# A two-block model on one core: the stick-breaking heads dealt among the portions of dense work, and the masked copy of the scores joined with its maximum

## What is computed

```python
def _stick_breaking_mixer(h, w_in, w_out):       # h: 256 x 1024, w_in: 1024 x 3072, w_out: 1024 x 1024
    q, k, v = [a.reshape(B, S, H, DH) for a in jnp.split(h @ w_in, 3, axis=-1)]     # 8 heads of 128
    z = jnp.einsum('bqhd,bshd->bhqs', qc, k) * scale
    mask = s_idx[None, :] < t[:, None]
    log_beta = jax.nn.log_sigmoid(z)
    log_one_minus = jnp.where(mask, jax.nn.log_sigmoid(-z), 0.0)
    between = lax.cumsum(log_one_minus, axis=3, reverse=True) - log_one_minus
    a = jnp.where(mask, jnp.exp(log_beta + between), 0.0)
    return (a @ v) @ w_out
```

## Time and profile before

| | us |
|---|---|
| median of 3 runs | 3481.79 (3479.11 to 3485.41) |
| profiled execution: its own time | 3479.61 |
| its span (first to last instruction) | 3477.9 |
| PE busy in it | 3281.5 (94%) |
| DVE, ACT, POOL busy | 1991.3, 1636.0, 205.3 |

### The profile page before, as it was taken

One profiled execution on the slowest core, in us unless ns is written; L12 is line 12 of the kernel. 1 busy time (PEld: TensorE's weight loads), 2 busy tenths in 40 slices (PEclk: granted clock), 3 DMA queues, 4 the chain that ended last, 5 costly groups with the idle time before them and its releaser, 6 DMA issues.

```text
span 3477.9 us, 51810 instructions
## 1 busy us (share of the span) xinstructions
PE 3281.5 (94%) x19397; PEld 2849.5 (82%) x19397; DVE 1991.3 (57%) x2821; ACT 1636.0 (47%) x2448; POOL 205.3 (6%) x247
## 2 busy tenths in 40 slices
PE   6998999998999999999998999899969998999899
PEld 5976988976988978898976987688758877887797
DVE  5555556565556656556655556755545555555663
ACT  4444444444444445444444445544444446445553
POOL 1010001000001000101011001000001000101100
PEclk9998999999999999999998999899989999999999
DMA  6653556542555643555653655145505550555364
GB/s 205 193 184 98 182 187 188 186 156 86 170 184 181 193 157 105 162 192 179 193 185 97 199 182 183 49 162 189 179 33 167 190 170 1 170 182 168 111 200 152
DMA packets 405035, 551.98 MB, mean 159 GB/s; under 512 B 33936, under 2 KB 247008, under 8 KB 404864
## 3 DMA queue, kind: packets, MB, share of 16 engines
q1 hardware_dynamic: 401056, 536.10, 47.9%
q0 software_dynamic: 2976, 10.81, 0.9%
q10 hardware_dynamic: 832, 2.74, 0.2%
HBM read 548.47 MB, written 1.05 MB: 158 GB/s over the span
## 4 chain that ended last, share of the span: by engine, by line
PE 84%; DVE 10%; ACT 3%; issue 1%; DMA 1%; POOL 0%; SPq 0%; DVEq 0%; ACTq 0%
PE G L768 15%; PE G L772 15%; PE G L769 15%; PE G L869 10%; PE G L871 10%; PE G L870 10%; DVE ring_lo_sb L1814 4%; PE T L744 2%; PE G L1250 1%; PE O L993 1%; PE S L965 1%; DVE act_hi_sb L1828 1%; DVE act_lo_sb L1838 1%; ACT ring_hi_sb L1317 1%; DVE x_sb L1996 0%
## 5 line engine op out<-in xcount | busy, mean ns | idle before, releaser
L1814 DVE TENSOR_TENSOR ring_lo_sb<-ring_sb,ring_hi_sb 128x1024 fp32r<-128x1024 f32 (+1 forms) x996 | 1207.9, 1228 | 661.0 <-ACT ring_hi_sb L1317 641.7
L1317 ACT ACTIVATE ring_hi_sb<-ring_sb 128x1024 fp32r<-128x1024 f32 (+1 forms) x1028 | 1060.6, 1045 | 792.3 <-DMA ring_sb<-ffn_w_down 223.9
L869 PE MATMUL G<-act_hi_sb,ring_hi_sb 128*128 128x256 f32 x3072 | 855.1, 278 | 0.0
L871 PE MATMUL G<-act_hi_sb,ring_lo_sb 128*128 128x256 f32 x3072 | 853.0, 278 | 0.0
L870 PE MATMUL G<-act_lo_sb,ring_hi_sb 128*128 128x256 f32 x3072 | 852.9, 278 | 0.0
L768 PE MATMUL G<-ring_hi_sb,hid_hi_sb 128*128 128x512 f32 x1456 | 586.1, 403 | 17.5 <-DVE hid_hi_sb L1847 5.1
L769 PE MATMUL G<-ring_lo_sb,hid_hi_sb 128*128 128x512 f32 x1456 | 582.1, 400 | 0.0
L871 PEld LDWEIGHTS G<-act_hi_sb,ring_lo_sb 128*128 128x128 f32 x3072 | 576.5, 188 | 0.0
L869 PEld LDWEIGHTS G<-act_hi_sb,ring_hi_sb 128*128 128x128 f32 x3072 | 576.5, 188 | 0.0
L870 PEld LDWEIGHTS G<-act_lo_sb,ring_hi_sb 128*128 128x128 f32 x3072 | 576.5, 188 | 0.0
L772 PE MATMUL G<-ring_hi_sb,hid_lo_sb 128*128 128x512 f32 x1344 | 534.6, 398 | 0.0
(11 more groups left out here) (243 smaller groups left out, 2533.8 us busy)
## 6 DMA issues: line engine op xcount, KB each, us to landing
ring_sb<-ffn_w_gate_up SPq DMA_DIRECT2D x704, 256.0 KB, 3.9
ring_sb<-ffn_w_down SPq DMA_DIRECT2D x352, 256.0 KB, 3.7
ring_sb<-mlp_w_up SPq DMA_DIRECT2D x256, 256.0 KB, 3.7
ring_sb<-mlp_w_down SPq DMA_DIRECT2D x256, 256.0 KB, 3.7
ring_sb<-a_w_in SPq DMA_DIRECT2D x48, 256.0 KB, 4.0
ring_sb<-sb_w_in SPq DMA_DIRECT2D x48, 256.0 KB, 4.1
ring_sb<-moba_w_in SPq DMA_DIRECT2D x48, 256.0 KB, 4.0
ring_sb<-w_mem_kv SPq DMA_DIRECT2D x32, 256.0 KB, 4.1
```

Of the source, the lines that this page charges most:

```text
L869: mm(dst, hi, act_hi[:, kt, :], start=(kt == 0 and f == 0), stop=False, skip_group_check=True)
L871: last = mm(dst, lo, act_hi[:, kt, :], start=False, stop=(kt == KT - 1), skip_group_check=True)
L1317: fn(ring_hi[:, s_, :, 0:w], ring[:, s_, :, 0:w], ACT.Copy).then_inc(hi_ready, 1)
L1814: v.tensor_tensor(ring_lo[:, s_, :, 0:w], ring[:, s_, :, 0:w], ring_hi[:, s_, :, 0:w], ALU.subtract).then_inc(lo_ready, 1)
```

## The change

1. **The stick stage becomes a `fused` one.** `FUSED_CHUNKS["stick"]` has the two chunks of values first (row-major, as before) and then four chunks that hold queries and keys of two heads each. These four are computed with the weights stationary (`turned_cell`), so queries and keys stand channel-major in `proj` and are used from there: the transposes and ACT's copies of them fall away. Chunk 2 comes ahead of the heads, chunks 3, 4, 5 in steps 0 to 5, the output projection from step 6 on (`DEAL["stick"]`), four cells per step. Heads still go in pairs. In an even step PE does the sums (`remaining`) of the last two heads, then the scores of the next; in an odd step its scores and then both outputs of the last pair.
2. **Its tiles shrink to 128 x 384** (`TRI`), without the part that is masked away; the sums go to the PSUM banks of the transposes (`T`); the multiplication L2429 goes.
3. **`score` is joined**: one `tensor_tensor_reduce` per half of the rows, out = (scores + mask) * (-scale), with the minimum as second output; two per head in place of four (masked) or two (unmasked). ACT takes exp with scale -1. POOL negates the scale for normed heads with one more instruction (`rsqrt(..., negative=True)`).
4. **`split_limits`**: in the last three steps of every fused stage the limit is max(touched[last], the last limit) + 1 and no longer the last limit + 3. This gives 27, 28, 29 where 29, 32, 32 stood for mix_b; 31, 32, 33 for 31, 34, 36 in mix_c and moba; 39, 40, 41 for 41, 44, 44 in nsa.
5. nsa: the multiplication with `cmp_any` moves out of each head's `place` (L2045, 8 times) to one place ahead of the heads (2 instructions).

```diff
+            "stick": [[(2 * D, HALF)], [(2 * D + HALF, HALF)]] + [[(p * GRP, GRP), (D + p * GRP, GRP)] for p in range(4)],
...
+        DEAL["stick"] = [("in", 2, BOTH, -1, -1), ("in", 3, BOTH, 0, 1), ("in", 4, BOTH, 2, 3), ("in", 5, BOTH, 4, 5),
+                         ("out", 0, BOTH, 6, 6), ("out", 1, BOTH, 6, 6), ("out", 2, BOTH, 7, 7), ("out", 3, BOTH, 7, 7),
+                         ("out", 4, BOTH, 8, 8), ("out", 5, LOWER, 8, 8), ("out", 5, UPPER, 9, 9)]
+        TRI = SEQ + P
...
-                limits.append(min(touched[min(s + 2, last)], full) if s < last - 2 else min(full, limits[-1] + 3))
+                limits.append(min(touched[min(s + 2, last)], full) if s < last - 2
+                              else min(full, max(touched[last], limits[-1]) + 1))
...
+                def turned_cell(j, par, slot, u):
+                    for k in range(UNIT_K):
+                        kt = UNIT_K * u + k
+                        for f in range(2):
+                            wide = slice((2 * j + f) * P, (2 * j + f + 1) * P)
+                            to, hi, lo = G[:, j, par, f * SEQ:(f + 1) * SEQ], ring_hi[:, slot, k, wide], ring_lo[:, slot, k, wide]
+                            mm(to, hi, act_hi[:, kt, :], start=(kt == 0 and f == 0), stop=False, skip_group_check=True)
+                            mm(to, hi, act_lo[:, kt, :], start=False, stop=False, skip_group_check=True)
+                            last = mm(to, lo, act_hi[:, kt, :], start=False, stop=(kt == KT - 1), skip_group_check=True)
+                    return last
+                def remaining(h):
+                    prepared()
+                    bank, j = t_open(c["T"]), h % 2
+                    mm(bank[:, 0:SEQ], from_on, pt[:, j, 0:SEQ], start=True, stop=False, skip_group_check=True)
+                    mm(bank[:, P:SEQ], ones, pt[:, j, SEQ:TRI], start=False, stop=True, skip_group_check=True)
+                    mm(bank[:, SEQ:TRI], from_on, pt[:, j, SEQ:TRI], start=False, stop=True, skip_group_check=True)\
+                        .then_inc(t_full, 1)
...
+                def stick_step(step):
+                    past = [step // 2 * 2 - 2, step // 2 * 2 - 1] if step >= 2 else []
+                    if step % 2 == 0:
+                        for h in past:
+                            remaining(h)
+                    if step < n_heads:
+                        if "taken" in heads[step]:
+                            for t in range(TT):
+                                pe.wait_ge(g_taken[t], g + heads[step]["taken"])
+                        stick_score(step)
+                    if step % 2:
+                        for h in past:
+                            stick_weigh(h)
...
+                for t in range(TT):
+                    w = N_CMP if h["k"][0] == "cmp" else P if h["mask"] and t == 0 else SEQ
+                    dst, src, top = sc[:, b, t, 0:w], S[:, t, 0:w], mx[:, col + t:col + t + 1]
...
+                    ins = v.tensor_tensor_reduce(dst, src, add, scales[t], BIG, ALU.add, ALU.min, top)
                 ins.then_inc(s_taken, 1)
                 dve.wait_ge(s_taken, base + j + 1)
-                v.tensor_reduce(mx[:, col:col + TT], dst, AX_X, ALU.max, negate=True)\
-                 .then_inc(mx_ready, 1)
+                dve.sem_inc(mx_ready, 1)
...
                     if step < n_steps:
                         ahead(n + limits[step])
                         finished(cut[step])
+                    if kind == "stick":
+                        stick_last(step)
```

More of the change, by code:

```diff
@@ L41 @@
 NEG = -1e30
+BIG = 3e38
 SCALE1 = DH1 ** -0.5
@@ L692, in plan @@
                 return mem + hs
+            if kind == "stick":
+                return [dict(taken=3 + h // 2) if h % 2 == 0 else {} for h in range(H2)]
             if kind == "moba":
@@ L1116, in fused @@
                     dense(lead)
-                for step in range(n_heads + 4):
+                for step in range(steps_of(kind, n_heads)):
+                    if kind == "stick":
+                        stick_step(step)
+                        dense(cut[step])
+                        turn_y(step)
+                        continue
                     if step < n_heads:
@@ L1500, in fused @@
                         hooks[step, "sums"]()
-                    if 0 <= step - 1 < n_heads:
+                    if 0 <= step - 1 < n_heads and kind != "stick":
                         exps(heads[step - 1], step - 1, base)
@@ L1760, in _ @@
                     per = -(-CONV_W // DIAGS)
-                    c["mixf"] = H2 * sum(k == "stick" for k, *_ in stages[:s]) + sum(k == "mix_a" for k, *_ in stages[:s])
+                    c["mixf"] = sum(k == "mix_a" for k, *_ in stages[:s])
                     for g in range(2, len(diag_groups) + per):
@@ new lines, in stick_last @@
+                def stick_last(step):
+                    if step % 2 and step < n_heads:
+                        for h in (step - 1, step):
+                            sc_ = sc[:, h % 2, :, :].rearrange("p t n -> p (t n)")[:, 0:TRI]
+                            dve.wait_ge(fn_out, c.up("fn_out"))
+                            v.scalar_tensor_tensor(pt[:, h % 2, 0:TRI], sc_, 0.0, pt[:, h % 2, 0:TRI], ALU.max,
+                                                   ALU.add).then_inc(prep_ready, 1)
@@ new lines, in fused @@
+                n_steps = steps_of(kind, n_heads)
+                for step in range(n_steps + 1):
+                    if kind == "stick":
+                        stick_first(step) if step < n_steps else None
+                    else:
+                        if 0 <= step - 1 < n_heads:
+                            score(heads[step - 1], step - 1, base)
+                        if step < n_heads and turns(heads[step]):
+                            c.up("T")
+                        if 0 <= step - 3 < n_heads:
+                            c.up("T")
+                        if kind == "mix_c" and step == 2:
+                            c.up("T")
+                        if 0 <= step - 4 < n_heads:
+                            place(heads[step - 4], step - 4, base)
+                    if step < n_steps:
@@ L2401, in lead @@
                     dve.wait_ge(fn_out, c.up("fn_out"))
+                    for t in range(TT):
+                        ins = v.tensor_scalar(gates[:, t, 0:H2], gates[:, t, 0:H2], cmp_any[:, t:t + 1], None, ALU.mult)
+                    link(ins)
                     done()
```

275 lines of the change are left out of this document (117 added, 158 removed).

## The result

The changed kernel's median is 3433.95 us (4 runs, 3424.85 to 3437.46) against 3483.6 for the kernel before (4 runs, 3479.11 to 3488.7): a ratio of 0.9847, 95% interval 0.9823 to 0.987. Timed again on another chip it gave 0.9859 (0.9835 to 0.9882). The profiled execution took 3433.15 us, with a span of 3431.3. That is 1.5% faster, 50 us, where 61 were forecast.

What follows compares the result with a forecast made beforehand. PE, busy 94% of the span, bounds the kernel, leaving its waits and lower-clock stretches; gains 40.6 + 11.7 + 4 + 6 - 1 = 61.3 us off 3479.6 give 3418.3, median 3420 us, range 3402 to 3444 (own range 3405 to 3434).

Steps and rivals of the forecast that it cites:

- Stick: Stick stage: falls from 166.1 to 125.5 us, a gain of 40.6 us (36 to 47).
- logs and banks: Stick steps 2, 4, 6: PE waits for `stick_last` and a bank, 5.0 us together; step 8 for the bank, 0.7.
- output copies: Stick steps 3, 5, 7: the second output waits 1.1 us each for DVE; step 9 waits 0.6.
- step 0's copy: Stick step 0: PE waits 1.0 us for the copy of chunk 2.
- last turn: Stick's last turn of the result: PE waits 1.6 us for ACT and DVE.
- opening and splits: Stick's opening and the splits of chunk 2: 2.5 us of waiting.
- second rival: Stick: splits in DVE's queue hold PE up, three times 5 us plus clock; stage 147, total about 3442; chance 0.18.
- long chain through ACT: Stick, between scores and sums: about 4.9 us through DVE and ACT, hidden under 7.5 us of PE work.
- Limits: Ends of nsa, mix_b, moba, mix_c: fewer splits ahead save 4.6, 4.6, 1.5, 1.0 us; gain 11.7 (0 to 14).
- Clock: Nsa and mix_b: with waiting gone, part of the time at 1.2 GHz goes too; gain 4 us (0 to 8).
- Joined scores: 72 heads outside stick: masked pair takes 0.86 us for 1.40; gain 6 us (0 to 15), POOL's negation loses 1.
- Its own signs of being wrong: Wrong if a stick step waits for splits, 1.2 GHz spells stay in the stage, or the two mix_a stages change.

Runs made afterwards that it cites:

- the last version: Changed kernel plus four small stick edits, with `stick_last` also moved ahead of its step's splits; 3421.88 us (5 runs), ratio 0.9808 to the kernel before; stick plus MLP 312.5 us.
- the runs with old ones: Two runs with separate scores: changed kernel with old scores (first mix_a 110.1 us), and stick change alone, old scores and limits elsewhere (first mix_a 109.9 us).

## Why the prediction came out as it did

- **Stick: right mechanism, size off by 11 us.** Forecast 125.5. On the same footing (together less 185.9) it is 136.5. The step that failed is "the same count for moba's work gives 109 us against 125.6 measured ... so I take 125.5": I had seen that the count from below misses 16 us in a like stage, and added 0.9. With the 16 added it would have been 140.6. What it missed, by terms: waits 18.1 instead of 14.7; 6.8 us at 1.2 GHz, worth 3.4, instead of none; and PE's own work, which with no spell is 126.6 - 11.9 = 114.7 in the last version, 4.8 above the 109.9 worked out from pitches. No single term has it. From start to start in that version's trace, waits left out, the dense products take 91.7 us where 89.3 were counted, the heads' products 18.8 (17.1) and the turnings 4.0 (3.5).
- **The waits one by one**, forecast and measured: logs and banks 5.7, 3.5; output copies 3.9, 5.2; step 0's copy 1.0, 0.8; last turn 1.6, 1.4; opening and splits 2.5, 3.6; the boundary 0, 3.4. Without the boundary the waits come to 14.7, as forecast, but by errors that cancel: the logs too high, the output copies and the splits too low. The boundary was not in the sum at all: unlike moba, the table deals upper cells to the last steps, so little is left to cover the addition and the norm.
- **The second rival** (splits in DVE's queue hold the heads) was right in kind, at one step instead of three: 1.6 us and a spell. The long chain through ACT is hidden, as forecast: in step 1 the logs end at 2502.92, before PE's chunk does at 2503.6. A table load takes 1.28 us, it starts 0.01 after the ACTIVATE before it ends, and the next ACTIVATE starts 1.30 after its start (2500.68 and 2501.98), as in the earlier trace rows; the further drain that the Trainium skill (ScalarE: Activation LUTs, What ACT_TABLE_LOAD costs) gives is not seen here.
- **Limits**: 11.7 forecast, 11.8 measured with the clock in it. The agreement of the sums is luck: mix_c gave more (2.8 for 1.0), nsa 5.6 for 4.6, mix_b less (3.7 for 4.6), moba none.
- **Clock** in nsa and mix_b: forecast 4, as a gain that follows from shorter waits, and for mix_b this step failed. Nsa lay at 1.2 GHz for 23.9 and 30.7 us in the two profiles that hold it as before, and for 13.7 to 20.5, 18.8 in the mean, in the ten that hold it as changed. In mix_b it was 13.7 and 17.1 before and 13.7 to 23.9, 20.1 in the mean, after, though PE waited 4.1 to 4.9 us less. At half weight that is some 4 us won and 2 lost. It is a part of why mix_b gave 1.5 us where 5 were named as a sign. Why mix_b has more spells is open.
- **Joined scores**: the masked pair was forecast at 0.86 us; the groups give 0.291 + 0.420 + 2 x 0.083 = 0.88, less the overlap seen above. The gain is 10.1, forecast 6 less 1 for POOL. Where it falls was judged worse: moba has 4.4 of it; mix_b and mix_c, with 16 heads each, none in their lengths, though in mix_b some 2 us of waiting went. The two instructions that the Trainium skill (VectorE: DVE Perf Modes, Two Vector instructions with no wait between them) gives for such an operation are there, but the second is 83 ns, not the 187 that I took from ACT.
- **mix_a** was given nothing and changed by 1.8 and 2.0 us; the first has it from the scores, which the runs with old ones show (110.1 and 109.9). For the second it is open: the two profiles that hold it as before, 125.4 and 124.1, differ by 1.3 themselves.
- **The sum.** Mixers but stick gave 22.7 (20.7 forecast), stick 29.6 (40.6): 9 too much. The rest is the base. The profiled execution before had two of eight feed-forward stages at the slow pitch, the one after had five: 3 x 3.4 = 10 us that have nothing to do with the change. 3418.3 + 9 + 10 = 3437; measured 3433, since nsa was 2.1 us shorter in this profile than in the mean of three. The sign that these stages stay "unchanged within 0.5 us" failed for this reason.
- **Its own signs of being wrong.** All three came: a stick step waited for splits (2.6 us in step 0), spells at 1.2 GHz stayed (two of 3.4 us), and the mix_a stages changed. The median of 3433.95 lies at the very end of the forecast's own range, 3405 to 3434: too much from stick was in part made good by too little from the scores.

## What to carry to other kernels

When heads are dealt among dense cells, each engine's queue should be laid out with the thing that PE needs next ahead of the splits, and the end of the stage needs cells left over for the addition and the norm. A count from below that misses a like stage by 16 us should be corrected by that much before it is used: here that gives 140.6 for the 136.5 measured. Judge an edit of a few us by its own stage in the profile, over more than one profile, and read PE's idle time and the time at 1.2 GHz apart: idle time repeated to 0.4 us in nsa, the spells did not repeat, and a few us more of them hide the gain of a removed wait.

## What was not expected of the hardware

- Feed-forward products of 256 columns follow each other every 40.0/355 = 0.113 us or every 40.0/342 = 0.117 us, for nearly a whole stage, at a granted clock of 1.00 with PE never idle. Which one changes from profile to profile of the same program: in 14 profiles 65 of 112 such stages were slow. One costs 3.4 us (184.9 against 188.3), so eight of them could make 27 us; 11.5 were seen between profiles of the changed kernel. That the spread of the unprofiled runs, 15 and 19 us, comes from it too is likely but not shown. The MLP stages had the slow pitch in all 14 profiles. What decides is open.
- The joined copy and minimum costs no more time than the copy (420 against 414 ns for 128 x 256), and the read of the minimum behind it, 83 ns, does not hold up the next instruction.
- Ten profiles of the same nsa stage have the same waits to 0.4 us and between 13.7 and 20.5 us at 1.2 GHz.
